# Norm boundaries of a two-block model: the second norm's sum of squares taken from sums over the output, and one pass over the tiles instead of two

## The reference

```
h = rms_norm(x, g_pre_mix) * (1 + sc_mix) + sh_mix
y = mixer(h)
x = x + gt_mix * rms_norm(y, g_post_mix)
h = rms_norm(x, g_pre_mlp) * (1 + sc_mlp) + sh_mlp
f = square(relu(h @ w_ff1)) @ w_ff2
x = x + gt_mlp * rms_norm(f, g_post_mlp)
```

## Time and profile before

| | |
|---|---|
| three runs, us | 2626.3, 2634.15, 2635.93 |
| median | 2634.15 |
| the profiled execution, its own time | 2624.85 |
| its span, first to last instruction | 2623.1 |
| busy: PE, DVE, ACT, GpSimd | 2502.1, 1261.5, 971.4, 1106.6 |
| granted TensorE clock, mean | 0.945 of full |

### The profile page before, as it was taken

One profiled execution on the slowest core, in us unless ns is written; L12 is line 12 of the kernel. 1 busy time (PEld: TensorE's weight loads), 2 busy tenths in 40 slices (PEclk: granted clock), 3 DMA queues, 4 the chain that ended last, 5 costly groups with the idle time before them and its releaser, 6 DMA issues.

```text
span 2623.1 us, 29172 instructions
## 1 busy us (share of the span) xinstructions
PE 2502.1 (95%) x10670; PEld 1926.1 (73%) x10670; DVE 1261.5 (48%) x1995; ACT 971.4 (37%) x1538; POOL 1106.6 (42%) x559
## 2 busy tenths in 40 slices
PE   5988899999999999899999999999999999999998
PEld 4875568678888678666868888867766668788886
DVE  6799655652452579955442211255556323311212
ACT  3357353332233245744333322335433322422322
POOL 3578412434344549751344444443430004444443
PEclk7999899999999999999999999999995569999999
DMA  6522102534543423210213323313220003222332
GB/s 235 187 80 73 49 25 81 192 121 152 184 159 121 131 80 97 66 59 23 70 51 97 93 91 96 96 48 92 82 81 1 1 17 97 81 90 94 96 95 74
DMA packets 215213, 239.75 MB, mean 91 GB/s; under 512 B 9738, under 2 KB 188746, under 8 KB 215114
## 3 DMA queue, kind: packets, MB, share of 16 engines
q1 hardware_dynamic: 215114, 238.45, 28.6%
HBM read 236.32 MB, written 2.10 MB: 91 GB/s over the span
## 4 chain that ended last, share of the span: by engine, by line
PE 81%; DVE 11%; ACT 1%; issue 1%; POOL 1%; DVEq 0%; POOLq 0%; ACTq 0%
PE product L2042 22%; PE product L2044 22%; PE product L2043 22%; DVE side L1488 5%; PE side L2490 3%; PE product L2512 2%; PE side L2500 1%; PE side L2297 1%; PE product L2321 1%; PE side L2088 1%; PE side L2095 1%; PE side L2102 1%; DVE slot_r L1589 1%; PE side L2315 1%; POOL slot_f L813 1%
## 5 line engine op out<-in xcount | busy, mean ns | idle before, releaser
L804 POOL TENSOR_TENSOR ring_low<-ring_f,ring_high 128x1024 fp32r<-128x1024 f32 (+1 forms) x350 | 841.4, 2408 | 1302.9 <-ACT ring_high L893 1302.7
L2042 PE MATMUL product<-slot_r,ring_high 128*128 128x512 f32 x2792 | 1120.1, 401 | 39.1 <-DVE slot_r L1420 9.3
L2043 PE MATMUL product<-slot_r,ring_low 128*128 128x512 f32 x2792 | 1107.4, 397 | 0.0
L2044 PE MATMUL product<-slot_r,ring_high 128*128 128x512 f32 x2792 | 1107.1, 397 | 0.0
L2042 PEld LDWEIGHTS product<-slot_r,ring_high 128*128 128x128 f32 x2792 | 527.4, 189 | 190.4 <-issue 35.3
L893 ACT ACTIVATE ring_high<-ring_f 128x1024 fp32r<-128x1024 f32 (+1 forms) x350 | 368.1, 1054 | 696.9 <-DMA ring_f<-in_w_ff 332.0
L2044 PEld LDWEIGHTS product<-slot_r,ring_high 128*128 128x128 f32 x2792 | 527.1, 189 | 126.3
L2043 PEld LDWEIGHTS product<-slot_r,ring_low 128*128 128x128 f32 x2792 | 527.5, 189 | 123.6 <-issue 1.2
L1457 DVE SCALAR_TENSOR_TENSOR va<-product,sqt 128x512 f32<-128x512 f32 x96 | 66.2, 690 | 389.4 <-ACT sqt L947 389.3
L1488 DVE SCALAR_TENSOR_TENSOR side<-slot_f,cols,side 128x512 f32<-128x512 f32 x332 | 220.6, 745 | 0.0
L1467 DVE TENSOR_TENSOR slot_f<-product,slot_f 128x512 f32<-128x512 f32 x64 | 44.2, 691 | 224.6 <-PE product L2044 224.5
(11 more groups left out here) (249 smaller groups left out, 2063.4 us busy)
## 6 DMA issues: line engine op xcount, KB each, us to landing
ring_f<-in_w_ff SPq DMA_DIRECT2D x128, 512.0 KB, 3.6
slot_f<-in_w_ada SPq DMA_DIRECT2D x48, 1024.0 KB, 6.4
ring_f<-in_w_in SPq DMA_DIRECT2D x96, 512.0 KB, 3.7
ring_f<-in_w_out SPq DMA_DIRECT2D x40, 512.0 KB, 3.4
ring_f<-in_w_up SPq DMA_DIRECT2D x32, 512.0 KB, 3.7
ring_f<-in_w_down SPq DMA_DIRECT2D x32, 512.0 KB, 3.4
slot_f<-in_x SPq DMA_DIRECT2D x4, 512.0 KB, 9.6
ring_f<-in_w_v SPq DMA_DIRECT2D x4, 512.0 KB, 3.8
```

What stands on the lines that cost most here:

```text
L804: pool.tensor_tensor(ring_low[:, s, :, 0:n], ring_f[:, s, :, 0:n], ring_high[:, s, :, 0:n].bitcast(F32), ALU.subtract).then_inc(low_ready. ...
L2042: pe.matmul(out_ap, high, rhs_high, start=start, stop=False)
L2043: pe.matmul(out_ap, low, rhs_high, start=False, stop=False)
L2044: return pe.matmul(out_ap, high, rhs_low, start=False, stop=stop)
```

## The change

**PE, first product of a part.** A quad takes two pairs together: for each input tile, four output tiles. It is used for the first two pairs of every MLP group (of the second block too), of the first projection of each layer and of the second block. The chunks are loaded in the quad's order. The prefetch of ACT goes to 6 chunks around a boundary, chunk 3 before the first high part of h, chunks 4 and 5 after the last.

```diff
+CHAINED = 6
...
+EARLY = 6
...
+def quad(self, n):
+    self.chunk(2)
+    self.chunk(2)
+    self.chunk(2, [(0, n), (1, n + 1)])
+    self.chunk(2, [(0, n + 2), (1, n + 3)])
+def hidden_group(self, n):
+    self.quad(n)
+    for p in range(2, FF_CHUNKS // 2):
+        self.pair(n + 2 * p)
```

```diff
+def sum_outputs(place, b, t):
+    n = 2 * (CHAINED - 1) * b + 2 * (t - 1)
+    wait(pool, place, y_sq, NT * b + t + 1)
+    if t > 1:
+        wait(pool, place, y_sums, n - 1)
+    pool.tensor_tensor(out_square(b, 0), out_square(b, 0), out_square(b, t), ALU.add).then_inc(y_sums.sem, 1)
+    wait(pool, place, yg_sq, CHAINED * b + t + 1)
+    if t > 1:
+        wait(pool, place, y_sums, n)
+    pool.tensor_tensor(gained_square(b, 0), gained_square(b, 0), gained_square(b, t),
+                       ALU.add).then_inc(y_sums.sem, 1)
...
 for i in range(I_OUT + AHEAD + HEADS, I_FF):
     low_part(place, LAYER, i)
-sum_squares(place, 1)
-sum_squares(place, 2)
-with pool.Fori(0, FF) as g:
-    for i in range(I_FF, I_FF + FF_CHUNKS):
+    if i >= I_FF - 4:
+        sum_outputs(place, 0, i - (I_FF - 5))
+sum_outputs(place, 0, 5)
+for i in range(I_FF, I_FF + AHEAD):
+    low_part(place, LAYER, i)
+wait(pool, place, hz_ready, NT)
+pool.memset(region_f[:, SE:SE + SLOT], 0.0).then_inc(y_cleared.sem, 1)
+with pool.Fori(0, FF - 1) as g:
+    for i in range(I_FF + AHEAD, I_FF + AHEAD + FF_CHUNKS):
         low_part(Place(l, g), LAYER, i)
-sum_squares(place, 3)
+for i in range(I_FF + AHEAD, I_FF + FF_CHUNKS):
+    low_part(Place(l, FF - 1), LAYER, i)
+    if i >= I_FF + FF_CHUNKS - 4:
+        sum_outputs(place, 1, i - (I_FF + FF_CHUNKS - 5))
+sum_outputs(place, 1, 5)
+following, plan = Place(l + 1), LAYER if l + 1 < LAYERS else SECOND
+for i in range(AHEAD):
+    low_part(following, plan, i)
```

```diff
+def output_stats(place, b, slot, gain, ready, weights):
     for t in range(NT):
+        if t < CHAINED - 1:
+            weights(t)
+        ready(t)
+        act.activation(out_square(b, t), tile(slot, t), ACT.Square).then_inc(y_sq.sem, 1)
+        if t < CHAINED:
+            act.activation(gained_square(b, t), tile(slot, t), ACT.Square, scale=gain(t)).then_inc(yg_sq.sem, 1)
+        if CHAINED - 1 <= t < NT - 1:
+            weights(t)
+    square_root_next()
+    wait(act, place, y_summed, b + 1)
+    deviation(place, y_totals, D, y_root)
+    weights(NT - 1)
+    wait(act, place, x_summed, b + 1)
+    deviation(place, x_sums, D, x_root, BLK)
...
+def split_high(place, n, ahead, move=None):
+    for t in range(NT):
+        if t == 0:
+            ahead.upto(place, AHEAD + 1)
         wait(act, place, hv_ready, 8 * n + t + 1)
```

```diff
+def residual_product(place, b, slot, gain, t):
+    if t == 0:
+        steps.did(dve.scalar_tensor_tensor(cross(b, 0), tile(slot, 0), gain(0), X[:, 0, :], ALU.mult, ALU.mult))
+    elif t < CHAINED:
+        if t > 1:
+            steps.wait()
+        steps.did(dve.scalar_tensor_tensor(cross(b, 1), tile(slot, t), gain(t), X[:, t, :], ALU.mult, ALU.mult))
+        steps.wait()
+        ins = dve.tensor_tensor(cross(b, 0), cross(b, 0), cross(b, 1), ALU.add)
+        if t < CHAINED - 1:
+            steps.did(ins)
+        else:
+            ins.then_inc(cross_ready.sem, 1)
+    else:
+        dve.scalar_tensor_tensor(cross(b, t), tile(slot, t), gain(t), X[:, t, :], ALU.mult,
+                                 ALU.mult).then_inc(cross_ready.sem, 1)
...
+def boundary(place, b, slot, n, gain, gain_next, move):
+    sums, v, q = PM[3], root[:, 3 * BLK:4 * BLK], root[:, 4 * BLK:5 * BLK]
+    by_kind = sums[:, 0:2 * BLK].rearrange("p (s k) -> p k s", k=2)
+    r_out, r_x, u = inv_cols[:, 0:BLK], inv_cols[:, BLK:2 * BLK], root[:, 2 * BLK:3 * BLK]
+    x0 = 8 * (b + 1)
+    def scaled(t):
+        steps.did(dve.tensor_tensor(tile(slot, t), tile(slot, t), rb_out, ALU.mult))
+    def moved(t):
+        dve.scalar_tensor_tensor(X[:, t, :], tile(slot, t), gain(t), X[:, t, :], ALU.mult,
+                                 ALU.add).then_inc(x_ready.sem, 1)
+    def value(t):
+        wait(dve, place, x_ready, x0 + t + 1)
+        if t >= 2:
+            wait(dve, following, hs_ready, 8 * n + t - 1)
+        dve.scalar_tensor_tensor(va[:, t % 2, :], X[:, t, :], gain_next(t), rb,
+                                 ALU.mult, ALU.mult).then_inc(hv_ready.sem, 1)
+    def low(t):
+        wait(dve, following, hh_ready, 8 * n + t + 1)
+        if move is not None:
+            ins = dve.scalar_tensor_tensor(tile_r(SB_, t), va[:, t % 2, :], move(t), tile_r(SA, t).bitcast(F32),
+                                           ALU.add, ALU.subtract)
+        else:
+            ins = dve.tensor_tensor(tile_r(SB_, t), va[:, t % 2, :], tile_r(SA, t).bitcast(F32), ALU.subtract)
+        ins.then_inc(hs_ready.sem, 1)
+    following = Place(place.layer + b)
+    wait(dve, place, y_root, b + 1)
+    settled(dve)
+    steps.did(dve.tensor_scalar(v, by_kind[:, 0, :], 1.0 / D, EPS, ALU.mult, ALU.add))
+    inverse_root(v, q, root[:, 0:BLK], r_out, y_rstd)
+    wait(dve, place, y_rstd, b + 1)
+    steps.did(dve.tensor_tensor(u, by_kind[:, 1, :], r_out, ALU.mult))
+    steps.wait()
+    wait(dve, place, cross_summed, b + 1)
+    steps.did(dve.scalar_tensor_tensor(u, PB[1][:, 0:BLK], 2.0, u, ALU.mult, ALU.add))
+    steps.wait()
+    steps.did(dve.tensor_tensor(u, u, r_out, ALU.mult))
+    steps.wait()
+    steps.did(dve.tensor_tensor(x_sums, u, x_sums, ALU.add))
+    steps.wait()
+    dve.tensor_scalar(x_sums, x_sums, 0.0, None, ALU.max).then_inc(x_summed.sem, 1)
+    wait(dve, place, x_summed, b + 1)
+    steps.did(dve.tensor_scalar(v, x_sums, 1.0 / D, EPS, ALU.mult, ALU.add))
+    wait(dve, place, y_spread, b + 1)
+    scaled(0)
+    wait(dve, place, x_root, b + 1)
+    settled(dve)
+    inverse_root(v, q, root[:, BLK:2 * BLK], r_x, x_rstd)
+    moved(0)
+    wait(dve, place, x_spread, b + 1)
+    for t in range(NT):
+        value(t)
+        if t < NT - 1:
+            scaled(t + 1)
+            steps.wait()
+            moved(t + 1)
+        low(t)
+def mlp_group(place, plan, o0, k0, between=None, dst=lambda t: tile(SE, t), final=None):
```

```diff
+def use_quad(place, plan, i, o, slots, need):
+    for k in range(NT):
+        need(k)
+        for m in range(4):
+            c = i + 2 * (k // KC) + m // 2
+            s, kk, at = chunk_slot(c), k % KC, m % 2 * P
+            if kk == 0 and m % 2 == 0:
+                wait(pe, place, low_ready, plan.split(c))
+            if k == 0:
+                wait_bank(pe, place, o + m)
+            ins = product(bank(o + m)[:], ring_high[:, s, kk, at:at + P], ring_low[:, s, kk, at:at + P],
+                          tile_r(slots[0], k), tile_r(slots[1], k), k == 0, k == NT - 1)
+            if kk == KC - 1:
+                ins.then_inc(done.sem, 1)
...
+def narrow(dst, at, step, src, moving, start=False, stop=False):
+    n = moving.shape[1]
+    for s in range(BLK):
+        c = at + step * s
+        ins = pe.matmul(dst[:, c:c + n], src[:, s * P:(s + 1) * P], moving, start=start and s == 0,
+                        stop=stop and s == BLK - 1)
+    return ins
...
+def chained_sums(place, b):
+    wait(pe, place, y_sums, 2 * (CHAINED - 1) * (b + 1))
+    narrow(PM[3], 0, 2, out_square(b, 0), ones[:, 0:1], start=True)
+    narrow(PM[3], 1, 2, gained_square(b, 0), ones[:, 0:1])
+    wait(pe, place, cross_ready, 3 * b + 1)
+    narrow(PB[1], 0, 1, cross(b, 0), ones[:, 0:1], start=True)
+def boundary(place, b, between=None):
+    for t in range(CHAINED, NT):
+        last = t == NT - 1
+        wait(pe, place, y_sq, NT * b + t + 1)
+        ins = narrow(PM[3], 0, 2, out_square(b, t), one_gain[:, b, t - CHAINED, :], stop=last)
+        if last:
+            ins.then_inc(y_summed.sem, 1)
+        wait(pe, place, cross_ready, 3 * b + t - CHAINED + 2)
+        ins = narrow(PB[1], 0, 1, cross(b, t), ones[:, 0:1], stop=last)
+    ins.then_inc(cross_summed.sem, 1)
+    if between is not None:
+        between()
+    wait(pe, place, y_rstd, b + 1)
+    spread(PM[1], inv_cols[:, 0:BLK]).then_inc(y_spread.sem, 1)
+    keep_busy(PB[0], 1)
+    wait(pe, place, x_rstd, b + 1)
+    spread(PM[2], inv_cols[:, BLK:2 * BLK]).then_inc(x_spread.sem, 1)
+    keep_busy(PB[0], 3)
```

```diff
 load_ada(l, unit_cols(ADA_GLU + p), ADA_GLU + p, SB_)
+if p == 3:
+    load_params(1)
```

439 lines of the change are left out of this document (242 added, 197 removed).

## The result

The changed kernel takes 2614.09 us (median of four, 2609.3 to 2616.46), the kernel before beside it 2633.45: ratio 0.9939, 95% interval 0.9925 to 0.9954. That is 16 us (12 to 20) where 34.5 were forecast.

A forecast was written before the change was run, and what follows sets the result against it. PE was taken to bound the kernel, with 81% of the chain, so gains lie only where it has no products. 46.7 - 12.6 + 6.4 - 6.0 = 34.5 us off the median 2634.15 gives 2599.7, so 2600 us; range 2578 to 2618.

The forecast's parts named there:

- off the gaps: At the four part boundaries, PE's stretches without products would shrink from 104.3 to 57.6 us, 46.7 us gained.
- clock: At the boundaries, with fewer filler matmuls, the clock may fall on new sums or first products: 1.5 us each, -6.0.
- quads: At a part's first products: +1.35 us at three boundaries, 0 at the fourth, +2.4 ahead of the last MLP; together +6.4.
- the prediction's own signs: Forecast wrong if boundary gaps are under 12 or over 17 us, PE waits in chained_sums, or MLP groups have grown.
- The steps of a gap: In each boundary gap, sums, second root, spread and first value make 11.3 us; port waits bring it to 14.0.
- I take no hold from it: In the middle boundaries, GpSimd's memset of 4096 columns, at most 5.0 us, would not hold DVE's operations.
- Rival B: At the boundaries, the memset holds DVE some 4.5 us in each middle one, low parts meet more: 2614 us, chance 0.16.
- So no wait, with little room, least in layer 0: Within a part's last chunk, chained_sums cost 3.15 us, -12.6 together, without PE waiting for GpSimd's additions or DVE.
- At nothing: Across the kernel, DVE's products with X, ACT's second squares, and parameter loads for layer 1 and the second block cost 0.
- A: At the boundaries, the port never meets the chain and the clock holds: gaps 11.3, gain 51, 2583 us, chance 0.22.
- D: In the 12 MLP groups, the ring starves the quads, 5 us a group: slower, 2660 us, chance 0.05.
- C: The clock is low throughout the boundaries: 25 us lost, gain 9, 2625 us, chance 0.11.

The follow-up runs named there:

- after_again: The changed kernel timed once more with no edit: 2613.91 us, ratio 0.9948 to the kernel before.
- chained_l0: Changed kernel with layer 0's middle token sums of tiles 0 to 5 moved behind the part's last product: 2612.69 us, 0.9938 to the kernel before.
- no_quads: Changed kernel with a part's first four output tiles taken and loaded as two pairs again: 2651.55 us, 1.0088 to the kernel before.

## Why the prediction was half right

By its own terms, the forecast and what the first profiles show:

| term | forecast | measured |
|---|---|---|
| off the gaps | 46.7 | 104.3 - 66.6 = 37.7 |
| chained_sums | -12.6 | last 48 longer by 10.1, 2.7, 4.3, 2.7: -19.7 |
| clock | -6.0 | inside the two terms above |
| quads: first 96 products at four boundaries and ahead of the last MLP | 6.4 | 2.1 x 3 + 0.2 + 2.0 = 8.5 |
| fourth chunk early | 0 | -2.2 - 2.2 = -4.4 |
| second block: PE's wait ahead of the fourth projection, 5.36 for 4.45 | 0 | -0.9 |
| sum | 34.5 | 21.2 |

Of the 13.3 us missing, the gaps are 9.0, chained_sums 7.1, the fourth chunk 4.4 and the second block 0.9; that nothing is to be added for the clock gives 6.0 back, the quads 2.1.

Against the second profile of before, with gaps of 100.0, the sum is 17. The runs' 16 (and the 14 of after_again) fit that, the more so with the 1.5 us of layer 0's first quad, which stand in no term. Between the two first profiles the spans show 8.4 only: the changed one lost 7.8 in layer 0's mixer, 5.5 of them not there in its second profile, and some 5 from the second block's projections to its last products, which before has in its second profile too. By the prediction's own signs it was wrong: two gaps over 17 (18.61 and 17.15), and PE waits in chained_sums. Its sign for the port came true: two-input steps of 1.7 to 2.3 us beside a low part, none beside the memset.

- **The steps of a gap** were right: layer 0's end, without a memset, has 13.92 us for 14.0, though its granted clock is 0.75. The low part of chunk 2 held the product step (1.81 for 0.16), that of chunk 3 moved(0) (2.86 for 0.75), both as foreseen.
- **The failed step: "I take no hold from it"**, the memset at nothing. It held a one-input step for 3.22 instead of 0.16 at both middle boundaries, 6.1 us together. I applied a rule on two-input operations and did not ask it of each form in the new chain, though the same section of the Trainium skill names one-input forms. Rival B had a price of 4.5 a boundary for it, 9 together. That the time met B's 2614 is luck: B has neither the wait in layer 0 nor the fourth chunk nor the quads' surplus. At the fourth boundary the low part fell on a refinement step (2.32) and not on moved(0) (0.74): from that step's start to the first value it takes 4.5 us there (1726.74 to 1731.23), 3.1 at layer 0's end, so 1.4 more.
- **The second failed step: "So no wait, with little room, least in layer 0"**. I counted DVE's products with X as covered and GpSimd's additions at 1.28; beside each other both took up to 1.7 (L1542 1.67, L888 1.71), and with a modulation unit of 6.4 us for every two tiles DVE was late at tile 5. Price: 10.1 us for 3.15, of it 2.7 waiting, 2.3 the sums' and some 2.4 the products' half clock. A part was cover: without the wait DVE is late at tile 7 instead, so chained_l0 gained 1.75 only.
- **Clock:** 6.0 was put on the first products. These ran at full clock (the fillers held it, 8 us at stake); what fell was the clock of the sums themselves. That chained_sums and clock as one sum, 18.6, come near the 19.7 measured for the last 48 is luck: layer 0's wait and half clock, which I had not foreseen, make 7 of it.
- **Quads:** the size was near (6.4 for 8.5), but I priced them as a part of their own, and so did the expectation of no_quads (8.5, measured 37): without them the change is slower than the kernel before. I also priced layer 0's first quad at nothing, and it seems to cost some 1.5.
- **"At nothing"** should have had the fourth chunk: I counted chunks 4 and 5 and missed that a low part ahead of the first high part of h meets DVE at two places where it had not been. 4.4 us.
- **The base:** my sum took its gaps from one execution; its two layer-end gaps held 1.7 us each that another execution lacks, by where the clock fell: at layer 0's end the four fillers ahead of the first spread took 3.41 us in the first profile and 1.97 in the second.

A fell, with no gap under 13.9, and D, with MLP groups behind a part's first one as before (89.37 us for 384 products, 92.03 in layer 0, in all kernels). C came in part: the clock's mean in the gaps is 0.60 to 0.80 for 0.81 to 0.93, but the products behind them start at full clock.
